# A two-block transformer kernel on one Trainium2 core: the opening taken by pairs of modulation chunks, and the merge of the two mixers regrouped

## The reference, cut to what matters

```python
mod = (jax.nn.silu(c) @ w_mod[l] + b_mod[l]).reshape(bsz, N_MOD, D_MODEL)
mc = (jax.nn.silu(c_ctx) @ w_mod[l] + b_mod[l]).reshape(N_MOD, D_MODEL)
hc = modulate(rmsnorm(ctx, g_mix[l]), mc[0], mc[1])        # context rows
h = modulate(rmsnorm(x, g_mix[l]), mod[:, 0, None], mod[:, 1, None])
# token_mixers: p = h @ w_in, split into gates f_f, f_b, values, q, og, u, v, ga, gb
merged = jax.nn.sigmoid(ga) * (o_a @ w_pa) + jax.nn.sigmoid(gb) * (o_b_mlp @ w_pb)
return merged @ w_o, s_f, s_b
```

## Time and profile before

| | |
|---|---|
| time, median of 3 runs | 1503.38 us (1501.32, 1503.38, 1507.06) |
| the profiled execution's own time | 1502.86 us |
| its span, first to last instruction | 1501.6 us |
| PE busy | 1448.4 us, 96% |
| DVE, ACT busy | 857.9 us (57%), 752.0 us (50%) |
| mean granted TensorE clock | 0.985 |
| mean HBM traffic | 178 GB/s |

### The profile page before, as it was taken

How to read it: one execution, slowest core, us unless ns; L and a number is a source line. 1 busy time by engine, 2 the same in 40 slices (tenths; PEclk the granted TensorE clock), 3 DMA queues, 4 the chain that set the end, 5 groups by cost and what they waited for, 6 DMA issues and landing times.

```text
span 1501.6 us, 19638 instructions
## 1 busy us (share of the span) xinstructions
PE 1448.4 (96%) x8098; PEld 1213.2 (81%) x8098; DVE 857.9 (57%) x1187; ACT 752.0 (50%) x1078; POOL 22.4 (1%) x72
## 2 busy tenths in 40 slices
PE   6899999989999999999999999999999999899998
PEld 4899689868888788888898788887888888788886
DVE  3636675685554665556454755657555465665543
ACT  3325353554454455544565654446545475555442
POOL 0000000000000000000021000000000000000000
PEclk8999899999999999999999999999999999999999
DMA  9237467545555565555533556555555551355552
GB/s 383 87 116 291 158 226 252 183 140 180 183 183 192 172 202 186 188 184 195 182 113 100 187 185 188 186 192 187 184 187 189 182 176 57 113 161 185 187 184 97
DMA packets 69930, 267.34 MB, mean 178 GB/s; under 512 B 7760, under 2 KB 8016, under 8 KB 66384
## 3 DMA queue, kind: packets, MB, share of 16 engines
q1 hardware_dynamic: 67680, 259.13, 51.6%
q10 hardware_dynamic: 2160, 6.95, 1.4%
HBM read 265.00 MB, written 1.05 MB: 177 GB/s over the span
## 4 chain that ended last, share of the span: by engine, by line
PE 87%; DVE 8%; ACT 3%; issue 1%; DMA 0%; SPq 0%; POOL 0%; DVEq 0%; ACTq 0%
PE PS L720 22%; PE PS L736 13%; PE PS L738 13%; PE PS L737 13%; PE PS L371 4%; PE PS L372 4%; PE PS L373 4%; DVE WL L1619 2%; PE PS L704 2%; PE PS L468 1%; PE PS L403 1%; PE PS L404 1%; PE PS L405 1%; DVE TN L2034 1%; PE PS L439 1%
## 5 line engine op out<-in xcount | busy, mean ns | idle before, releaser
L1619 DVE TENSOR_TENSOR WL<-RAW,WH 128x1024 fp32r<-128x1024 f32 (+1 forms) x440 | 531.7, 1220 | 332.9 <-ACT WH L1085 332.4
L1085 ACT ACTIVATE WH<-RAW 128x1024 fp32r<-128x1024 f32 (+1 forms) x440 | 453.7, 1054 | 293.8 <-DMA RAW<-in_up 172.4
L736 PE MATMUL PS<-WH,XH 128*128 128x512 f32 (+1 forms) x928 | 383.0, 413 | 14.3 <-DVE XL L2042 14.1
L738 PE MATMUL PS<-WH,XL 128*128 128x512 f32 (+1 forms) x928 | 363.8, 392 | 0.0
L737 PE MATMUL PS<-WL,XH 128*128 128x512 f32 (+1 forms) x928 | 363.6, 392 | 0.0
L736 PEld LDWEIGHTS PS<-WH,XH 128*128 128x128 f32 x928 | 175.4, 189 | 64.8 <-DVE XL L2042 19.2
L738 PEld LDWEIGHTS PS<-WH,XL 128*128 128x128 f32 x928 | 175.5, 189 | 37.5
L737 PEld LDWEIGHTS PS<-WL,XH 128*128 128x128 f32 x928 | 176.3, 190 | 28.1
L720 PE MATMUL PS<-WH,GH 128*128 128x512 f32 x440 | 137.4, 393 | 0.0
L720 PE MATMUL PS<-WL,GH 128*128 128x512 f32 x440 | 135.7, 390 | 0.0
L720 PE MATMUL PS<-WH,GL 128*128 128x512 f32 x440 | 135.7, 389 | 0.0
(11 more groups left out here) (343 smaller groups left out, 1832.1 us busy)
## 6 DMA issues: line engine op xcount, KB each, us to landing
RAW<-in_up SPq DMA_DIRECT2D x220, 512.0 KB, 4.7
RAW<-in_down SPq DMA_DIRECT2D x110, 512.0 KB, 3.3
RAW<-in_win SPq DMA_DIRECT2D x44, 512.0 KB, 6.4
RAW<-in_mod SPq DMA_DIRECT2D x16, 1024.0 KB, 6.7
MC<-in_mod SPq DMA_DIRECT2D x8, 1024.0 KB, 14.2
RAW<-in_sbqk SPq DMA_DIRECT2D x16, 512.0 KB, 4.7
GROW<-in_grow ACTq DMA_DIRECT2D x9, 512.0 KB, 4.2
RAW<-in_wo SPq DMA_DIRECT2D x8, 512.0 KB, 4.1
```

The costliest lines, as they stand in the source:

```text
L736: e.matmul(o_[:, 0:n], l, w[:, s], start=(k == 0), stop=False, skip_group_check=True)
L738: m = e.matmul(o_[:, 0:n], ll, w[:, s], start=False, stop=(k == KD - 1), skip_group_check=True)
L1085: e.activation(WH[s][:, 0:c], RAW[s][:, 0:c], ACT.Copy).then_inc(*sig("hi", j))
L1619: e.tensor_tensor(WL[s][:, 0:c], RAW[s][:, 0:c], WH[s][:, 0:c].bitcast(F32), ALU.subtract).then_inc(*sig("lo", j))
```

## The change

- **PE** takes the modulation chunks in the order 4, 0, 5, 1, then gate steps k = 0 to 3 of x, then the sums of ctx, then chunks 6, 2, 7, 3, then gate steps 4 to 7. The two PSUM banks of the gates are held out of the ring between.
- **ACT** copies the rows of the first eight chunks to `MR` (DVE did); its splits of `win` loads 0, 1 and 2, 3 and its squares of ctx move between these.
- **DVE** multiplies by the inverse root two row blocks at a time (`normed`), makes gains two columns at a time (`gains`: 16 small operations where 4 were), applies `modulated` to two row blocks, and does the low part (`low`) later, with other work in the gap.
- **SP** issues `MC` 4, 0, `win` 0, 1, `MC` 5, 1, XC, `win` 2, 3, `MC` 6, 2, 7, 3.
- **Merge:** DVE and ACT split `wo` 0 to 3 before the second pair of merged quarters (before: `wo` 3 after the last quarter). PE's and SP's parts of the merge are as they were.

SM and CST are the first loads in both kernels.

```diff
-        FIRST = (4, 5, 6, 7, 0, 1, 2, 3)
+        FIRST = (4, 0, 5, 1, 6, 2, 7, 3)
...
             sums("nx", 0, 4)
             mod_first(4)
             sums("nx", 4, 8)
+            mod_first(0)
             mod_first(5)
-            mod_first(6)
-            mod_first(7)
-            mods_finish()
-            mod_first(0)
-            mods_finish()
-            sums("nc", 0, 8)
             mod_first(1)
             mods_finish()
 
 
             step = gate_group(0, 0, 2)
-            for z in range(4):
-                step(2 * z)
-                step(2 * z + 1)
-                if z < 2:
-                    mod_first(2 + z)
-                    mods_finish()
+            for k in range(4):
+                step(k)
+            for c in range(2):
+                BANK.hold(("fg", 0, c))
+            sums("nc", 0, 8)
+            mod_first(6)
+            mod_first(2)
+            mods_finish()
+            mod_first(7)
+            mod_first(3)
+            mods_finish()
+            for k in range(4, 8):
+                step(k)
+            for c in range(2):
+                BANK.release(("fg", 0, c))
...
+            def mod_rows(i):
+                mr, before = MR.take(("mr", i), ("modt", i))
+                ac.wait_ge(*at("modp", i))
+                ac.wait_ge(*after(before))
+                e.activation(mr[:, :], BANK.of(("modp", i))[:, 0:T], ACT.Copy).then_inc(*sig("act", "mr", i))
+
...
             squares("nx", XF, (s_xf, 16))
             e.preload_act_table_set("sqrt_and_others")
+            mod_rows(4)
             root("nx")
+            mod_rows(0)
+            split(0)
+            mod_rows(5)
             modulated("h", XF, HH, 0)
+            split(1)
+            mod_rows(1)
+            modulated("h", XF, HH, 1)
             squares("nc", XC, (s_ctx, 16))
-            split(1)
+            split(3)
             root("nc")
-            modulated("h", XF, HH, 1)
-            split(3)
+            mod_rows(6)
+            mod_rows(2)
             modulated("h", XF, HH, 2)
+            mod_rows(7)
+            mod_rows(3)
             modulated("h", XF, HH, 3)
...
-            for which, kind in enumerate(("wpa", "wpb")):
-                for c in range(2):
-                    if which:
-                        for t2 in range(2):
-                            mt = 4 * c + 2 * t2
-                            ac.wait_ge(*at("mgd", "s", c, t2))
-                            e.activation(MH[:, mt:mt + 2, :], MG[:, mt:mt + 2, :],
-                                         ACT.Copy).then_inc(*sig("mh", 2 * c + t2))
-                    split_to(kind, c)
+            split_to("wpa", 0)
+            split(chunk["wo", 3])
+            for c in range(2):
+                for t2 in range(2):
+                    mt = 4 * c + 2 * t2
+                    ac.wait_ge(*at("mgd", "s", c, t2))
+                    e.activation(MH[:, mt:mt + 2, :], MG[:, mt:mt + 2, :], ACT.Copy).then_inc(*sig("mh", 2 * c + t2))
+                split(chunk["wo", 5 + c])
...
+            def gains(z):
+
+                mod_added(4 + z)
+                dv.wait_ge(*at("mod", 4 + z))
+                scale_of("va", 2 * z, S_GMIX + 2 * z, 8 + 2 * z, 0, 2)
+                scale_of("vc", 8 + 2 * z, S_GMIX + 2 * z, 8 + 2 * z, 1, 2)
...
-            mod_rows(5)
-            invert("nx", XF)
-            mod_rows(6)
-            mod_rows(7)
-            mods_finish()
-            dv.wait_ge(*at("mod", 7))
-            scale_of("va", 0, S_GMIX, 8, 0)
-            scale_of("vc", 8, S_GMIX, 8, 1)
-            mod_rows(0)
-            mods_finish()
-            modulated("h", XF, 0, 0, HH, HL, 0)
+            invert("nx")
+            normed("nx", XF, 0)
+            gains(0)
+            mod_added(0)
+            modulated("h", XF, 0, 0, 0)
+            split(0)
+            low("h", XF, HH, HL, 0)
             split(1)
-            mod_rows(1)
-            mods_finish()
-            modulated("h", XF, 0, 0, HH, HL, 1)
-            invert("nc", XC)
+            normed("nx", XF, 1)
+            gains(1)
+            mod_added(1)
+            modulated("h", XF, 0, 0, 1)
+            normed("nx", XF, 2)
+            low("h", XF, HH, HL, 1)
+            normed("nx", XF, 3)
             split(3)
-            mod_rows(2)
-            mods_finish()
-            modulated("h", XF, 0, 0, HH, HL, 2)
-            mod_rows(3)
-            mods_finish()
-            modulated("h", XF, 0, 0, HH, HL, 3)
+            invert("nc")
+            gains(2)
+            mod_added(2)
+            modulated("h", XF, 0, 0, 2)
+            normed("nc", XC, 0)
+            low("h", XF, HH, HL, 2)
+            gains(3)
+            mod_added(3)
+            modulated("h", XF, 0, 0, 3)
+            normed("nc", XC, 1)
+            low("h", XF, HH, HL, 3)
             for z in range(4):
-                modulated("hc", XC, 8, 1, HCH, HCL, z)
+                modulated("hc", XC, 8, 1, z)
+                if z < 2:
+                    normed("nc", XC, z + 2)
+                low("hc", XC, HCH, HCL, z)
             split(5)
...
+            first_gated(0, 0)
+            first_gated(0, 1)
+            split_to("wpa", 0)
+            first_gated(1, 0)
+            split(chunk["wo", 0])
+            first_gated(1, 1)
+            split(chunk["wo", 1])
+            merged(0, 0)
+            merged(0, 1)
+            split(chunk["wo", 3])
+            merged(1, 0)
+            split(chunk["wo", 4])
+            merged(1, 1)
+            scale_of("vf", 40, S_GFFN, 32, 0, 8)
...
-            modulation(4, 5, 6, 7, 0)
-            e.dma_start(XC[:, :, :], a["ctx"]).then_inc(s_ctx, 16)
+            modulation(4, 0)
             weights(0)
             weights(1)
-            modulation(1)
+            modulation(5, 1)
+            e.dma_start(XC[:, :, :], a["ctx"]).then_inc(s_ctx, 16)
             weights(2)
             weights(3)
-            modulation(2, 3)
+            modulation(6, 2, 7, 3)
```

More of the change, by code:

```diff
@@ L442, in pe_program, with mr_kept @@
             rows = []
+            def mr_kept(i):
+                return at("act", "mr", i) if i in FIRST else at("mr", i)
             def mods_finish():
@@ L448, in mods_finish @@
                     b, empty = bank(("modt", i), ("mod", i))
-                    pe.wait_ge(*at("mr", i))
+                    pe.wait_ge(*mr_kept(i))
                     pe.wait_ge(*empty)
@@ L461, in mod_chunk @@
             def mod_chunk(i, w, come):
-                b, empty = bank(("modp", i), ("mr", i))
+                b, empty = bank(("modp", i), ("act", "mr", i) if i in FIRST else ("mr", i))
                 pe.wait_ge(*come)
@@ L1625, in split_to, with invert @@
                 split(chunk[kind, i if kind == "mod" else 2 * i + 1] + 5)
-            def invert(nm, src):
+            def invert(nm):
                 rb = RB.of(("rb", nm))
@@ L1631, in invert, with normed, mod_added @@
                 e.reciprocal(rb[:, :], rb[:, :]).then_inc(*sig("dve", nm, "r"))
+            def normed(nm, src, z):
+                s = src[:, 2 * z:2 * z + 2, :]
                 dv.wait_ge(*at("dve", nm, "r"))
[L1633 to L1636, removed]
+                e.tensor_tensor(s, s, RB.of(("rb", nm))[:, :].unsqueeze(1).to_broadcast([P, 2, T]),
+                                ALU.mult).then_inc(*sig("dve", nm, z))
             rows = []
+            def mod_added(i):
+                dv.wait_ge(*at("modt", i))
+                b = BANK.of(("modt", i))
+                if i // 4 in (2, 5):
+                    n, c = i // 4 // 3, slice(i % 4 * T, i % 4 * T + T)
+                    dv.wait_ge(s_grow[n], 16)
+                    e.tensor_tensor(GROW[n][:, c], b[:, 0:T], GROW[n][:, c], ALU.add).then_inc(*sig("mod", i))
+                else:
+                    e.tensor_tensor(MOD[:, 2 * i:2 * i + 2, :], two(b[:, 0:4]),
+                                    SM[:, S_BMOD + 2 * i:S_BMOD + 2 * i + 2].unsqueeze(2).to_broadcast([P, 2, 2]),
+                                    ALU.add).then_inc(*sig("mod", i))
             def mods_finish():
                 while rows:
[L1642 to L1652, removed]
+                    mod_added(rows.pop(0))
             def mod_rows(i):
@@ L1665, in mods, with scale_of, modulated @@
                     split_to("mod", i)
[L1667 to L1678, removed]
+            def scale_of(name, dst, gcol, mcol, which, n):
+                e.tensor_scalar(VEC[:, dst:dst + n], MOD[:, mcol:mcol + n, which], 1.0, None,
+                                ALU.add).then_inc(*sig("dve", name, dst, "+"))
+                dv.wait_ge(*at("dve", name, dst, "+"))
+                e.tensor_tensor(VEC[:, dst:dst + n], VEC[:, dst:dst + n], SM[:, gcol:gcol + n],
+                                ALU.mult).then_inc(*sig("dve", name, dst))
+            def gains(z):
[3 more added lines that the diff above has]
+                scale_of("vc", 8 + 2 * z, S_GMIX + 2 * z, 8 + 2 * z, 1, 2)
+            def modulated(kind, src, av, which, z):
```

(26 more changed lines are left out.)

## The result

The changed kernel takes 1488.38 us at the median of 4 runs (1487.32 to 1493.78), against 1502.92 us for the kernel before on the same chip (4 runs, 1501.32 to 1507.06). The ratio is 0.9913, with an interval of 0.9889 to 0.9938: faster by 14.5 us. The forecast was 1487.3 us, its range 1480 to 1493. The profiled execution took 1487.32 us, which is also the shortest of the four, with a span of 1486.0: 15.6 us less than the 1501.6 of before.

A forecast was written before the change was run, and what follows sets the result against it. PE was taken as the bound, with its losses in the opening and one stop in the merge. 13.6 us and 2.5 us sum to 16.1 us, giving 1487.3 us against the median of 1503.38, range 1480 to 1493.

The forecast's parts named there:

- What bounds it: Whole kernel: PE, busy 96% of the span; what it saves before 60 us it saves at the end too.
- The opening: Before 60 us: the context gates' steps end at 57.6 us in place of 71.2, a gain of 13.6 us.
- the walk at full clock: Opening, step by step at full-clock prices: gate steps 0 to 3 end at 29.4 us, all steps at 57.6.
- rival 2: DVE and ACT's chain longer than walked, or clock falls in the opening's gaps: 4 to 8 us less gain; chance 0.17.
- The copy's price: Opening: ACT's copy of a row to MR taken as 0.47 us, on the path four times at most.
- ACT's ring of squares: Opening: ACT's eighth ctx square waits for PE's first ctx sum at about 29.9 us, with 6 us of cover.
- Loads: SP's queue: MC 6, 2, 7, 3 land at about 28.6 to 36.1 us, before use; smallest slack 1.8 us.
- Rival 3: Transfers decide: the four late MC loads land 5 us later, 3 us lost at two places; over 1495.9 us; chance 0.04.
- The merge: Output projection: PE's stop of 2.56 us behind the split of wo 3 goes, a gain of 2.5 us.
- The clock: Whole kernel: stop length alone doesn't decide clock falls; the sum could lose or gain a fall in any run.
- Rival 1: Clock's fall at 170 us, or one elsewhere, doesn't come: at most 6.7 us more gain, 1480.6 to 1484; chance 0.17.
- Rival 4: Opening: PE's short stops hold the clock at half, so slower; 1504 to 1521 us; chance 0.02.

The follow-up runs named there:

- e4: Changed kernel with x multiplied by its inverse root in four operations on end, ahead of the first gains; 1488.65 us median.
- e2: Changed kernel with the merge's blocks in their old order, so only the opening is changed; 1492.18 us median.
- e6: Changed kernel with DVE copying the row of modulation chunk 11 before the second direction's gate sums, not after; 1480.09 us median.
- e10: Changed kernel with the earlier copy of row 11 (e6), and the merge's blocks in their old order; 1486.43 us median.
- e8: Kernel before with only the earlier copy of row 11 by DVE, ahead of the second direction's gate sums; 1501.17 us median.
- e1: Kernel before with only the merge's new order on ACT and DVE; 1502.59 us median.
- e3: Kernel before with only the rows of chunks 2 and 3 copied by ACT, into two buffers of their own; 1496.49 us median.
- e9: Changed kernel with the eight copies of rows back on DVE, orders and pairs of gains kept; 1489.84 us median.
- e5: Changed kernel with the load of chunk 5 issued ahead of win 0 and 1; 1488.05 us median.

## Why the prediction was right

**What bounds it.** Right. Both kernels' mixers take 204.07 us, so what PE saved before 60 us arrived whole at 262 us. Where the time at half clock in the mixers changed, it didn't: e4's 1.4 us were gone there.

**The opening: 12.6 us for 13.6.** The term was a little too large in this execution, and the step is the walk at full clock. PE's first chunk took 1.07 us for the 1.81 of before, so it was through with chunk 0 by 15.4 us instead of 16.2, and stood 1.6 us for the load of chunk 5, where I had 0.3. The clock fell at 18.0 and came back at 28.3. Each turn of a row took 1.0 us for 0.61; gate steps 0 to 3 ended at 31.6 for 29.4. Part of it came back: the ctx sums took 3.6 us (I had 4.0), and the wait for row 7 was as walked. Steps 4 to 7 began at 41.3 for 40.3, and nothing changed after that. In e2, with the same opening program, chunk 0 was done at 16.3, the two waits for chunks 5 and 1 were 0.56 and 0.87 us, the clock fell at 20, and the opening gained 13.5 us, nearly the forecast; e6 and e10 gained 12.1 and 12.5. The one late microsecond of the forecast is this fall, which stood in rival 2 as one of its two causes; the other, longer hand-overs, hardly came: second low part 27.5 for 26.5, fourth 44.1 for 42.8.

**The copy's price** was 0.36 to 0.38 us for the 0.47 taken.

**ACT's ring of squares.** As predicted: the eighth square waits for PE's first ctx sum, and nothing waits for it.

```profile
32.27 0.42 ACT L1109 ACTIVATE SQ<-XC 128x256 f32<-128x256 f32 x1 [3.35 <-PE PS L439]
```

**Loads.** The four late chunks were there when PE came to them; no stop of PE between 30 and 40 us. Rival 3 has nothing for it, but before 20 us the load of chunk 5 did set a stop of 1.6 us, where the walk had 0.3 us for it and 0.8 for chunk 1.

**The merge: 2.86 us for 2.5.** Right, and PE had no stop at `wo` 5, for which the walk had 0.6 us of slack.

**Sum.** 15.5 us at the first update of x, for 16.1 forecast; 14.5 at the medians, whose difference from 15.5 is less than their scatter. That the time came within 1.1 us of the forecast has luck in it: the rest took 1189.4 and 1189.2 us in the two profiles, where others took over 6 us more, and of the changed kernel's four runs one, 1493.78 us, lies outside the stated range.

**The clock.** The prediction drew its width from it, and this is what the runs bear out most: the rest, the same work in all kernels, took from 1189.2 to 1195.7 us. Rival 1 was priced at 6.7 us at most for the fall alone; e6 and e8 measured 8.1 with the stop, 6.0 without. It did not come in the changed kernel. Rival 4 did not come: the longest stretch at half in any opening was 13.7 us (e8). Rival 4's remark that gaps under 1 us make no swing holds for the trace before, but not for every run: in the merge alone the clock fell at 1224 us behind gaps of at most 0.8 us.

## What to carry to other kernels

When a short copy hands work from one engine to the bottleneck, look at what stands ahead of it in its engine's list: copies of two rows, the first behind 6 us of DVE's work, held more than half of the opening's gain, and which engine got the eight copies in the end mattered by about 2 us. Cut profiles at markers before and after an edit, since a local gain of 3 us can be exact in its stretch and invisible at the median, when falls of the clock elsewhere move by as much. Compare several runs at equal mean clock as well, where medians differ by a few us. A stop of PE can cost more than its length, when the clock falls behind it: 2.1 us of stop cost 8.1 in the mixers.

## What the runs showed of the hardware

Stops of PE of about 2.5 us were followed by a half clock in some kernels and not in others at the same place of the program: the merge's stop kept the clock in the kernel before and in e2, and lost it in e8 and e10. The gaps near 1224 us, none longer than 0.8 us, kept it in the kernel before and lost it in e1. The Trainium skill ("TensorE: Matmul & The Clock Gate", Part 1) says that the activity window runs free of the kernel's start, which fits stops that keep the clock in one execution and lose it in another; no run here could set the phase, so that it is the cause is not shown.

How long the half clock lasts is no fixed figure, not even at one place, and a busy PE doesn't end it at once. In the mixers it was 13.7 us, or 10.2 in e3, e4 and e9, with PE busy in every slice of it behind the first. Near 1200 to 1232 us it was 3.4 or 6.8 us at a time in most kernels, but 13.7 in e4 and e5 and 13.6 in e10, again with PE busy (e4, stretches of PE):

```profile
1215.00:1220.00 5.00, 5.00 (x22) 0.50 0.00 0
1220.00:1225.00 5.00, 5.00 (x23) 0.50 0.31 102
```

Behind the mixers' stop come matmuls of small weight tiles (64*64, 128*64 and 128*32); the ones of e4 here have tiles of 128*128 throughout. So a long half clock isn't tied to small tiles. What keeps it down wasn't tried.
